# Tail tiles, norms and head tiles as one stage by parts of 256 tokens, in a three-layer transformer kernel

## The reference, cut to what matters

```python
h = modulate(rmsnorm(x, g_pre), shift, scale)      # x * (1 + scale) + shift
y = mixer_or_ffn(h)                                # its last step is a product @ w_out
x = x + gate * rmsnorm(y, g_post)
# the next h is again modulate(rmsnorm(x, ...)), and the next step again a product @ w_in
```

## Time and profile before

| | us |
|---|---|
| median of 3 runs (4785.26 to 4790.76) | 4789.85 |
| the profiled execution, its own time | 4782.46 |
| its span from first to last instruction | 4780.4 |
| PE busy | 4171.8 (87%) |
| DVE busy | 1185.3 (25%) |
| ACT busy | 849.6 (18%) |
| POOL busy | 332.1 (7%) |
| mean granted clock of TensorE | 0.937 |

### The profile page before, as it was taken

One profiled execution on the slowest core, in us unless ns is written; L12 is line 12 of the kernel. 1 busy time (PEld: TensorE's weight loads), 2 busy tenths in 40 slices (PEclk: granted clock), 3 DMA queues, 4 the chain that ended last, 5 costly groups with the idle time before them and its releaser, 6 DMA issues. The chain is left out here.

```text
span 4780.4 us, 35771 instructions
## 1 busy us (share of the span) xinstructions
PE 4171.8 (87%) x13196; PEld 2119.5 (44%) x13196; DVE 1185.3 (25%) x1859; ACT 849.6 (18%) x1633; POOL 332.1 (7%) x362
## 2 busy tenths in 40 slices
PE   6979699999968987997999699768889978999993
PEld 3545355555534443443444354545544444444441
DVE  1033333320030305104330312544330033111115
ACT  1024211100011112102110223513220021111110
POOL 0023100000010000000000002300000001111103
PEclk8989899999989999998999899979899988999996
DMA  5312211113241010221222114310012215999995
GB/s 224 110 58 88 93 53 48 53 46 133 98 157 64 31 50 0 70 70 48 79 67 81 55 49 164 126 53 23 31 36 75 71 58 216 402 412 414 389 389 210
DMA packets 134892, 584.86 MB, mean 122 GB/s; under 512 B 16688, under 2 KB 18736, under 8 KB 107136
## 3 DMA queue, kind: packets, MB, share of 16 engines
q1 hardware_dynamic: 103920, 478.15, 27.1%
q0 software_dynamic: 23088, 76.89, 4.2%
q10 hardware_dynamic: 7776, 28.32, 1.4%
HBM read 528.77 MB, written 66.06 MB: 124 GB/s over the span
## 5 line engine op out<-in xcount | busy, mean ns | idle before, releaser
L710 PE MATMUL ps<-arena 128*128 128x512 f32 (+1 forms) x2624 | 931.2, 518 | 26.4 <-POOLq L2697 23.0
L710 PEld LDWEIGHTS ps<-arena 128*128 128x128 f32 x2624 | 501.2, 191 | 455.8 <-issue 426.7
L589 PE MATMUL ps<-arena 128*128 128x512 f32 (+1 forms) x1408 | 473.9, 496 | 35.4 <-ACTq L2697 24.0
L498 PE MATMUL ps<-arena 128*128 128x512 f32 (+1 forms) x1120 | 474.2, 585 | 24.6 <-DVEq L2697 23.6
L2382 PE MATMUL ps<-arena 128*64 128x512 f32 (+1 forms) x1152 | 396.4, 620 | 34.8 <-DMA arena<-w_gate_up 33.0
L589 PEld LDWEIGHTS ps<-arena 128*128 128x128 f32 x1408 | 266.4, 191 | 248.0 <-issue 193.7
L661 PE MATMUL ps<-arena 128*128 128x512 f32 x768 | 336.9, 601 | 14.3 <-DVEq L2697 12.5
L498 PEld LDWEIGHTS ps<-arena 128*128 128x128 f32 x1120 | 213.3, 191 | 285.5 <-issue 257.5
L1403 PE MATMUL ps<-arena 128*128 128x512 f32 x640 | 277.3, 595 | 9.0 <-POOLq L2697 6.7
L2382 PEld LDWEIGHTS ps<-arena 128*64 128x64 f32 (+1 forms) x1152 | 151.0, 169 | 243.0 <-issue 240.5
L661 PEld LDWEIGHTS ps<-arena 128*128 128x128 f32 x768 | 147.7, 193 | 201.8 <-issue 185.1
(11 more groups left out here) (311 smaller groups left out, 3521.3 us busy)
## 6 DMA issues: line engine op xcount, KB each, us to landing
arena<-w_gate_up SPq DMA_DIRECT2D x144, 1024.0 KB, 16.4
arena<-ada SPq DMA_DIRECT2D x144, 512.0 KB, 5.4
arena<-w_down SPq DMA_DIRECT2D x72, 1024.0 KB, 13.1
arena<-ffn_in SPq DMA_DIRECT2D x88, 512.0 KB, 3.2
y_rows<-arena POOLq DMA_DIRECT2D x8, 4096.0 KB, 48.3
y_rows<-arena ACTq DMA_DIRECT2D x54, 512.0 KB, 8.2
arena<-ffn_out SPq DMA_DIRECT2D x32, 512.0 KB, 3.5
arena<-ret_qk SPq DMA_DIRECT2D x16, 512.0 KB, 5.0
```

The lines of the kernel that those rows point to most:

```text
L498: mm = pe.matmul(k.ps[:, 2 * s + t % 2, 0:w], lhsT=k.ring[:, u % SLOTS, (c % 8) * P:(c % 8 + 1) * P], rhs=self.rhs[:, c, o:o + w], start=c ...
L589: mm = pe.matmul(k.ps[:, 2 * s + t % 2, 0:w], lhsT=k.ring[:, u % SLOTS, (c % 8) * P:(c % 8 + 1) * P], rhs=self.rhs[:, c, o:o + w], start=c ...
L710: mm = pe.matmul(k.ps[:, 2 * s + j % 2, 0:w], lhsT=k.ring[:, u % SLOTS, c * P:(c + 1) * P], rhs=k.H[:, c, o:o + w], start=c == 0, stop=c = ...
```

## The change

- A stage `Seam` takes the place of both norms at the five places, with the last tiles of the product ahead (the tail, 5, 2, 3, 2 and 6 tiles) and the first tiles of the product behind (the head: 4 of ffn_in0, 8 of ret_qk, 4 of ffn_in1, 8 of dif_qk, and the shared expert's 4, which leave Router).
- Tokens go in parts of 256: two latent parts, and the context as a third at the first two places. PE does all tail tiles for part 0, then for part 1, and so on (a "phase" each), then the head tiles for part 0, and so on. The norms of a part run on ACT and DVE during the phase that follows its tail; PE puts the one matmul of the first norm's sum ahead of its matmul 5 of that phase, and the eight of the second norm's ahead of its matmul 27.
- ACT adds nothing up: it squares each tail tile out of PSUM and copies it, POOL adds the squares; squares of the earlier tiles are summed by DVE at the stage's start. The additions to X are DVE's (POOL has none).
- Results rotate over four PSUM banks instead of two. The tail's weights stay in the ring until the last part has used them.
- Modulations: hyb_qku now holds all of its 12 tiles in one stage and carries four sets; hyb_out and ret_qk carry none; ffn_out0 carries two in six tiles (one, two, one, one, three quarters), ret_out two in five tiles (two, two, two, two).
- A quarter's matmuls have 2 columns of weights instead of 32, and ACT copies a row in four pieces of two partitions.
- LoadContext moves ahead of the group norm of layer 1, and the context's norm of layer 2 is a stage of its own (`ContextNorm`) ahead of ffn_out1.
- Router's POOL multiplies the shared expert's halves ahead of the store of h_rows, not behind it.

```diff
 class ModSet:
...
             for j in range(4):
-                mm = pe.matmul(k.ps[32 * j:32 * j + 32, self.bank, :], lhsT=k.csil[:, self.cvec, c, :],
+                mm = pe.matmul(k.ps[32 * j:32 * j + 2, self.bank, :], lhsT=self.cvec[:, 2 * c:2 * c + 2],
                                rhs=k.ring[:, (u + j) % SLOTS, h * T:(h + 1) * T], start=c == 0, stop=c == KD - 1)
...
-        act.copy(self.row, k.ps[:, self.bank, :]).then_inc(k.sig("mod_row_ready").sem, 1)
+        for j in range(4):
+            a = act.copy(k.row[32 * j:32 * j + 2, :], k.ps[32 * j:32 * j + 2, self.bank, :])
+        a.then_inc(k.sig("mod_row_ready").sem, 1)
...
+class Seam(Stage):
+    SUM1, SUM2 = 5, 27
+    ROOT1, SQUARES, ROOT2, SHIFT = 6, 17, 28, 34
...
+        self.phases = [list(range(done, KD))] * np_ + [head.tiles(p) for p in range(np_)]
...
+    def tensor(self, pe):
...
+            for i, t in enumerate(tiles):
+                n = self.first[f] + i
+                if n >= 4:
+                    sem, count = self.left[n - 4]
+                    pe.wait_ge(k.sig(sem).sem, count)
+                for c in range(kt):
+                    m = i * kt + c
+                    if 1 <= f <= np_ and m == self.SUM1:
+                        first_sum(f - 1)
+                    if 1 <= f <= np_ and m == self.SUM2:
+                        second_sum(f - 1)
...
+                    if not tail and i == 0:
+                        pe.wait_ge(k.sig("part_normed").sem, self.normed + KD * p + c + 1)
+                    mm = pe.matmul(k.ps[:, n % 4, 0:w], lhsT=k.ring[:, u % SLOTS, (c % 8) * P:(c % 8 + 1) * P],
+                                   rhs=x[:, c, o:o + w], start=c == 0, stop=c == kt - 1)
...
+    def scalar(self, act):
...
+                    now = lambda m: min(m // kt, len(tiles)) == i
+                    if now(self.ROOT1):
+                        root(f - 1, 0)
+                    if now(self.SQUARES):
+                        squares(f - 1)
+                    if now(self.ROOT2):
+                        root(f - 1, 1)
+                    if now(self.SHIFT):
+                        shift(f - 1)
...
+                act.activation(self.sq[:, n % 4, :], src, ACT.Square).then_inc(k.sig("tail_squared").sem, 1)
+                act.copy(self.Yo[:, tiles[i], o:o + w], src).then_inc(k.sig("part_taken").sem, 1)
...
+    def gpsimd(self, pool):
...
+                acc = self.acc[:, o:o + w]
+                pool.tensor_tensor(acc, acc, self.sq[:, n % 4, :], ALU.add).then_inc(k.sig("tail_added").sem, 1)
...
+        def grow(c):
+            o, w, kind = self.parts[c]
+            layer, gain = self.post
+            rs = inverse(c, 0)
+            for h in range(2):
+                y = self.Yo[:, 4 * h:4 * h + 4, o:o + w]
+                own(dve.tensor_tensor(y, y, rs, ALU.mult))
+                for j in range(4 * h, 4 * h + 4):
+                    x = k.X[:, j, o:o + w]
+                    dve.scalar_tensor_tensor(out=x, in0=self.Yo[:, j, o:o + w], scalar=k.mods[:, layer, kind, gain, j:j + 1],
+                                             in1=x, op0=ALU.mult, op1=ALU.add).then_inc(k.sig("tokens_added").sem, 1)
...
+        def scale(c):
+            o, w, _ = self.parts[c]
+            rs = inverse(c, 1)
+            for h in range(2):
+                dve.tensor_tensor(self.xn[:, c % 2, 4 * h:4 * h + 4, :], k.X[:, 4 * h:4 * h + 4, o:o + w], rs, ALU.mult)\
+                    .then_inc(k.sig("scaled_ready").sem, 1)
...
 def plan(k, d):
...
-    add(ModLinear(k, d["hyb_out"], k.H, Yo, sets[1][0:2]))
-    add(Norm(k, Yo, 0, 2, scratch=F + 6144))
-    add(Norm(k, k.X, 0, 4, 3, k.H))
+    add(Linear(k, d["hyb_out"], 3, k.H, Yo))
+    add(Seam(k, d["hyb_out"], k.H, Yo, 3, (0, 2), (0, 4, 3), both, Head(k, d["ffn_in0"], 4, 3, tiles(raw)), F + 6144))
...
+    add(ModLinear(k, d["ffn_out0"], hid, [sets[1][2], sets[2][0]], quarters((1, 2, 1, 1, 3, 0)),
+                  (None, None, None, 0, None, 1), tiles(k.H)[0:6], kt=FT))
...
+    add(ModLinear(k, d["ret_out"], O, sets[2][1:3], quarters((2, 2, 2, 2, 0)), (None, None, 0, None, 1),
+                  tiles(Yo)[0:5], kt=16, spans=(LAT,)))
...
+    add(ContextNorm(k, load, 2, 1, 0, F + FT * N))
```

More of the change, by code:

```diff
@@ new lines, with __init__, gpsimd, tiles @@
+class Head:
+    def __init__(self, k, w, n, n_parts, dst, func=ACT.Copy):
+        self.k, self.w, self.n, self.n_parts, self.dst = k, w, n, n_parts, dst
+        self.func = func if isinstance(func, tuple) else (func,) * n
+    def gpsimd(self, pool): pass
+    def tiles(self, p):
+        return list(range(self.n))
+    def last(self, t):
+        return self.n_parts - 1
+    def turned(self, p, t):
+        return False
+    def take(self, act, p, t, src, o, w):
+        act.activation(self.dst[t][:, o:o + w], src, self.func[t]).then_inc(self.k.sig("part_taken").sem, 1)
@@ new lines, with __init__, tiles, last @@
+class TurnedHead(Head):
+    def __init__(self, k, w, dst, queries, n_parts, rope):
+        super().__init__(k, w, 8, n_parts, dst)
+        self.queries, self.rope = queries, rope
+    def tiles(self, p):
+        return list(range(8)) if p < 2 else list(range(self.queries, 8))
+    def last(self, t):
+        return 1 if t < self.queries else self.n_parts - 1
+    def turned(self, p, t):
+        return p < 2
+    def gpsimd(self, pool):
+        self.rope.gpsimd(pool)
+    def take(self, act, p, t, src, o, w):
+        if self.turned(p, t):
+            self.rope.turn(act, 8 * p + t, src)
+        else:
+            super().take(act, p, t, src, o, w)
+    def apply(self, dve, p, t, src, o, w):
+        self.rope.apply(dve, 8 * p + t, src, self.dst[t][:, o:o + w], self.k.sig("turned_part_taken").sem, o)
@@ L717, in scalar @@
         k = self.k
+        for j in range(0, len(self.head), 2):
+            act.wait_ge(k.sig("conv_done").sem, self.conv - len(self.head) + j + 1)
+            x = self.cv[:, j, 0:self.end]
+            act.activation(x, x, ACT.Silu).then_inc(k.sig("silu_done").sem, 1)
         def silu(i, j):
@@ L2594, in gpsimd, with __init__, scalar, vector @@
         pool.dma_start(k.X[:, :, T:N], self.dram["ctx2T"]).then_inc(k.sig("context_loaded").sem, 16)
-        pool.wait_ge(k.sig("context_loaded").sem, self.got + 16)
+class ContextNorm(Norm):
+    def __init__(self, k, load, layer, gain, shift, scratch):
+        super().__init__(k, k.X, layer, gain, shift, k.H, spans=(CTX,), which=(1,), scratch=scratch)
+        self.load = load
+    def scalar(self, act):
+        act.wait_ge(self.k.sig("context_loaded").sem, self.load.got + 16)
+        super().scalar(act)
+    def vector(self, dve):
+        dve.wait_ge(self.k.sig("context_loaded").sem, self.load.got + 16)
+        super().vector(dve)
+def split(items, counts):
+    at = [sum(counts[:i]) for i in range(len(counts) + 1)]
+    return [items[lo:hi] for lo, hi in zip(at, at[1:])]
 def plan(k, d):
```

399 lines of the change are left out of this document (281 added, 118 removed).

## The result

The changed kernel took **4630.08 us** (median of 4 runs, 4615.24 to 4637.23) against 4790.31 for the kernel before (4 runs), a ratio of 0.9666 (95% interval 0.9647 to 0.9686). The forecast was 4612, its range 4590 to 4652.

A forecast was written before the change was run, and what follows sets the result against it. PE bounds the kernel, busy 4171.8 of 4780.4 us. Places gain 189.4, other terms lose 11.8: 177.6 off the profiled 4782.5 gives 4604.9; the median lies 7.4 higher, so 4612, range 4590 to 4652.

The forecast's parts named there:

- 3. ret_out: Between ret_out and ffn_in1: 44.9 us gap and 1.9 slow start go; sums, boundaries and last part's wait come; gain 34.4.
- 4. ffn_out1, less the context's norm: Between ffn_out1 and dif_qk: 55.5 us gap and 1.9 go; sums, a boundary and the context's norm stage, 15.6, come; gain 33.1.
- 5. w_out2: Between w_out2 and Router: 45.0 us gap goes; sums, boundaries, last part's wait, shared expert's tiles and ring load come; gain 3.1.
- LoadContext as a stage: LoadContext as a stage of its own would cost 1.0 us, about the price of any new stage boundary.
- The chain: One part's norms, from its last tail matmul: last square at 11.8 us, ready to multiply at 20 to 23.4 us.
- 2.7 us at each: At ret_out and w_out2 the last part's chain outlasts its one head phase, so PE waits 2.7 us at each.
- pairs and triple: Quarters sharing a tile wait for the ring: ten pairs at 2.4 us each, one triple at 4.9; 9.9 lost.
- DVE and POOL hold each other up: Rival: POOL's additions delay DVE's work, every chain comes 3 us late, 12 parts cost 36: 4648 us; chance 0.15.
- The ring starves: Rival: ten pairs wait twice as long for the ring and the triple 8 us, +27: 4639 us; chance 0.08.
- Router gives nothing back: Rival: Router's later steps wait for something else that took as long, so its gain is lost: 4637 us; chance 0.05.
- Narrow matmuls in series: Rival: quarters' matmuls with 2 columns of weights run one by one, not four abreast, 175 us more: 4787; chance 0.03.
- Slower by the clock: Rival: many short waits keep TensorE at 1.2 GHz in the five stages, doubling their PE work: 5110 us; chance 0.02.

The follow-up runs named there:

- the last place alone: Changed kernel with the two norms restored at the first four places and LoadContext back in its old place; moved modulations stay: 4771.30 us, 0.9977 of the kernel before.
- late sums: Changed kernel with second sums, second root and shifts four matmuls later (31, 32, 38 for 27, 28, 34): 4639.54 us, 0.9698 of the kernel before.
- all edits: Changed kernel plus LoadContext beside the group norm, second sums five matmuls earlier, context's norm inside ffn_out1, quarters spread: 4580.28 us, 0.9581 of the kernel before.
- the spread one: Changed kernel with ffn_out0's quarters as 2, 1, 2, 1, 2 instead of 1, 2, 1, 1, 3: 4623.16 us, 0.9656 of the kernel before.
- early sums: Changed kernel with second sums five matmuls earlier (22 for 27) and shifts from 30 instead of 34: 4602.25 us, 0.9638 of the kernel before.

## Why the forecast was right in kind, and 18 us too low

I compare the two profiled executions stretch by stretch. Where a product also changed its modulations, they are taken out: the eight quarters with their waits were 21.3 us of hyb_out and 22.5 of ret_qk (hyb_out with its two norms took 162.45 us before and 141.15 in the run with the last place alone, where it carries no modulations; ret_qk took 97.15 and 74.60); they are 27.9 of ret_out's five tiles, 22.7 more in hyb_qku and 6.2 more in ffn_out0, the slower records behind the triple's wait of 4.20 included.

| step of the forecast | forecast, us | measured, us |
|---|---|---|
| 1. hyb_out | 43.3 | 42.8 |
| 2. ffn_out0 | 50.7 | 51.1 |
| 3. ret_out | 34.4 | 32.7 |
| 4. ffn_out1, less the context's norm | 33.1 | 34.1 |
| 5. w_out2 | 3.1 | 1.6 |
| Router | 24.8 | 24.9 |
| modulations, with the boundary won | -9.0 | -13.0 |
| three more copies in the opening stage | -1.8 | -1.4 |
| LoadContext as a stage | -1.0 | -8.0 |
| sum of what the change touches | 177.6 | 164.8 |
| stages that it does not touch | 0 | -19.8 |

The last two make the 145.0 us between the spans. How a stage's time is shared out between its place and its modulations is uncertain by about 1 us; the sums are not.

- **Gaps and prices.** Right. In the rows of ACT's copies at hyb_out (L910, at 578.57, 582.02 and 585.48) one head tile of 256 columns follows another at 3.45 us; two take 6.9, as one of 512 does. The Trainium skill's fixed 2.5 ns for each matmul (TensorE: Matmul & The Clock Gate, "Wait — 56ns, not 53.3ns?") does not show: cutting tiles cost nothing that the rows tell.
- **The chain.** Right to 0.1 us but for the sum's wait. The lag at hyb_out was 0.9 and not 1.6, the last part's wait 2.1 and not 2.7.
- **Failed in size: "2.7 us at each"** for the last part. I priced the wait and not what comes behind it: 2.1 of wait and 1.8 behind it, 1.4 of these the clock's, 3.9 at each: 1.2 of the 1.7 and of the 1.5 that places 3 and 5 lack.
- **Failed in size: "LoadContext as a stage of its own: 1.0".** It cost 8.0, 6.2 of wait and 1.8 of slow records behind it. I took the price of a boundary from boundaries where no engine had just issued a transfer. The row of its one DMA instruction is 0.91 us long, but POOL was late at the meeting by 6. The trace of the kernel before shows these 6 us at LoadContext's old place, where they were part of the 55.5 that place 4 counts as gone; I did not look. Moving its POOL part into a stage with other work gave the 8.0 back.
- **Failed in size: pairs and triple.** The waits grew by 12.7 us (19.0 to 31.7) and not by 9.9, though the triple cost 5.9 with its two waits, near the 4.9 taken; in all 13.0 are lost where 9.0 were forecast. Each pair waits 1.5 to 1.8 for ada, and up to 1.3 more for the tile behind it, where 2.4 for both was charged.
- **The context's norm.** Right: 14.2 of gap (17.8 against 3.6) and 1.7 of slow start (ffn_out1's first 264 records took 116.4 us, 114.7 at the pace of before), 15.9 in place of 15.6. The run with it inside ffn_out1 shows that 11 of it was avoidable.
- **Rivals.** *DVE and POOL hold each other up*: they do, but for 0.1 to 0.4 us of a part, not 3. *The ring starves*: no, the longest wait is 4.2. *Router gives nothing back*: it gave 24.9. *Narrow matmuls in series*: 1.90 us a quarter. *Slower by the clock*: mean clock 0.943, but the mechanism is there in small, as the run with late sums shows.
- **Not in the forecast at all: stages that no edit touches.** They took 19.8 us more in the profiled execution: 9.9 from layer 2's K product to w_out2, 5.9 in Router's later part and the experts, the rest in the stages of both other layers.

The largest of these can be read. Layer 2's scan has the same matmuls in both kernels. PE at one of its chunks (L2098 begins a chunk, L1021 is its convolution's product), in the changed kernel and then in the run with the last place alone:

```profile
3123.92 44.28 PE L1021 MATMUL ps<-arena 128*128 128x512 f32 x128 [0.87 <-DVEq L3035]
3205.56 41.55 PE L1021 MATMUL ps<-arena 128*128 128x512 f32 x128 [0.87 <-DVEq L3035]
```
```profile
3269.23 41.55 PE L1021 MATMUL ps<-arena 128*128 128x512 f32 x128 [0.87 <-DVEq L3032]
```

The granted clock at the start of either:

```profile
3115.00:3132.00 17.00, 15.48 (x55) 0.60 0.01 1
3132.00:3168.00 36.00, 36.00 (x117) 1.00 0.14 44
```
```profile
3260.00:3277.00 17.00, 14.34 (x82) 1.00 0.00 0
```

The same 128 records take 44.3 or 41.6 us, by whether the clock had fallen in the sparse work ahead of them (it is 0.55 in the 8.9 us ahead of the 44.28, and 1.00 ahead of the other). Over the ten traces of this study the stretch behind the K product up to the last product but one ahead of w_out2 (2719.2 to 3624.0 in the changed kernel) took 896.5 us in the kernel before, in the last place alone and with all edits (the same to 0.1 us chunk by chunk), 896.1 with late sums, 904.8 in both profiles of the changed kernel and in the spread one, 890.8 with early sums, 900.9 and 903.9 in the others. So it is not noise of each chunk but a pattern that an execution falls into, worth up to 14 us. What picks it stays open; both profiles of the changed kernel have the same slow one, and the kernel before shares one with the fastest kernel here.

The two profiled executions differ by 15 us less than the medians do (one is 7.9 below its median, the other 7.2 above), so of the 19.8 us 15 can be the choice of executions. Against the medians the forecast was 18 too low: 13 by its own terms, above, and some 5 by the rest. Whether those 5 belong to the change in any way stays open; they are less than the spread of one kernel. No errors cancel here: every term that missed by more than 1 us came out dearer than forecast.

## What to carry to other kernels

Two norms between two products can be hidden almost wholly by running the tail and the head of the products in parts of the tokens, if each part is ready before TensorE comes to its head tiles. The last part has only one phase of matmuls over its chain (24 us here), so it is the one to compute by the row. Most waits of 2 us or more inside such a stream cost 1.6 to 2.7 us above their length here, so that putting a sum, a root and the shifts a few places earlier gave back more than the wait in the row. An almost empty stage is not free: give its one DMA to an engine's part of a stage that has work, and look in the trace you already have for how late that engine comes.

## What was unexpected of the hardware

- **POOL is late behind a DMA that it issues.** The instruction's row is 0.91 us, the meeting of all engines right behind it was held up for 6 us, in both kernels and as long as the load of 1 MB took to land (5.9 us).
- **What is lost behind a wait does not grow with it.** Behind waits of 0.91 us: nothing. Behind 2.1: 1.8 us eight times, 0.4 or 0.5 three times. Behind 3.61: 2.5 and 2.1. Behind 4.53: 2.6. Behind 5.95: 1.6 (64 records in 15.60, with 14.0 at the pace of 44 in 9.66). Behind the 7 us at the group norm: 1.8 to 2.7 in six traces.
- **Untouched stages fall into one of several patterns of the clock**, 890.8 to 904.8 us for the same work. Two executions of this kernel can't be compared to better than some 10 us without looking at the clock of the stretches that did not change.
